# Head 7's searches ahead of its rows, eight rows ahead of its gates, no unit search or gelu inside the map stage, four tiles between heads 6 and 7

## What is computed

```
def peer_mixer(h, wq, subkeys, u, v):
    q = (h @ wq).reshape(B, S, PEER_HEADS, 2, PEER_HALF_DIM)          # 8 heads
    scores = jnp.einsum('bshcd,hcnd->bshcn', q, subkeys)               # 2 x 128 keys
    s_top, i_top = lax.top_k(scores, PEER_TOPK)                        # 16 of 128, twice
    cand = s_top[..., 0, :, None] + s_top[..., 1, None, :]             # 16 x 16 sums
    cand_idx = i_top[..., 0, :, None] * PEER_N_KEYS + i_top[..., 1, None, :]
    best, pos = lax.top_k(cand, PEER_TOPK)                             # 16 experts a head
    expert_idx = jnp.take_along_axis(cand_idx, pos, axis=-1)
    gates = jax.nn.softmax(best, axis=-1)
    a = jnp.einsum('cd,ced->ce', h, u[expert_idx])
    act = jax.nn.gelu(a, approximate=False) * gates
    return jnp.einsum('ce,ced->cd', act, v[expert_idx])
```

## Time and profile before

| | us |
|---|---|
| three runs, median | 3875.9 |
| three runs, lowest and highest | 3874.65, 3895.38 |
| the profiled execution | 3852.57 |
| its span | 3850.8 |
| TensorE busy | 3490.0 (91%) |
| VectorE busy | 2636.5 (68%) |
| GpSimd busy | 1382.5 (36%) |
| ScalarE busy | 982.7 (26%) |

### The profile page before, as it was taken

The page is one execution under the profiler, slowest core; times in us unless marked ns, Lnnn a source line. Parts: engine busy times, 40 slices in busy tenths (PEclk is TensorE's granted clock), DMA queues, the critical chain, the costliest instruction groups (busy, mean ns, idle before and its releaser), DMA issues.

```text
span 3850.8 us, 50373 instructions
## 1 busy us (share of the span) xinstructions
PE 3490.0 (91%) x13726; PEld 2235.0 (58%) x13726; DVE 2636.5 (68%) x5617; ACT 982.7 (26%) x2147; POOL 1382.5 (36%) x1220
## 2 busy tenths in 40 slices
PE   4998998999956999999978989989997689999997
PEld 2554445776754448874445544467767544688643
DVE  6656016898898777677566640289899987777774
ACT  1433102322263003330023330123323610133200
POOL 0000002444424565566400000044454256566662
PEclk9999999999978999999989989999998889999999
DMA  6322215888756999899942322178877589999997
GB/s 239 140 103 77 98 61 188 322 311 313 275 180 241 404 401 390 330 388 388 374 183 104 109 85 90 61 260 331 313 286 260 180 306 401 402 377 337 390 392 296
DMA packets 274015, 999.71 MB, mean 260 GB/s; under 512 B 31353, under 2 KB 48249, under 8 KB 262785
## 3 DMA queue, kind: packets, MB, share of 16 engines
q0 software_dynamic: 153600, 553.72, 38.2%
q1 hardware_dynamic: 120194, 443.42, 30.5%
HBM read 971.85 MB, written 25.17 MB: 259 GB/s over the span
## 4 chain that ended last, share of the span: by engine, by line
PE 65%; DVE 22%; issue 4%; DVEq 4%; DMA 3%; ACT 2%; ACTq 0%; POOL 0%; SPq 0%; POOLq 0%
PE ps L605 23%; PE ps L558 12%; PE ps L785 9%; DVE mod L1431 4%; DVE arena L1425 4%; PE ps L516 3%; PE ps L548 3%; PE ps L613 3%; PE ps L493 2%; DMA arena<-in_u_dram,idx 2%; PE ps L636 1%; DVE mod L1445 1%; PE ps L525 1%; PE ps L589 1%; DVE arena L1321 1%
## 5 line engine op out<-in xcount | busy, mean ns | idle before, releaser
L1167 POOL DMA_INDIRECT arena<-in_u_dram,idx x512 | 656.1, 1281 | 984.7 <-issue 652.3
L558 PE MATMUL ps<-hT,mod 128*128 128x256 f32 x4096 | 929.0, 381 | 0.0
L605 PE MATMUL ps<-arena 128*128 128x512 f32 x2048 | 881.5, 594 | 3.7 <-ACT hT L963 3.7
L1167 POOL DMA_INDIRECT arena<-in_v_dram,idx x512 | 630.2, 1231 | 632.2 <-DVE mod L1431 369.6
L558 PEld LDWEIGHTS ps<-hT,mod 128*128 128x128 f32 x4096 | 762.4, 191 | 92.1
L1425 DVE CUSTOM_DVE_ANT_0 arena<-arena 128x1024 f32<-128x1024 f32 x512 | 617.1, 1226 | 232.7 <-DMA arena<-in_u_dram,idx 229.5
L1431 DVE SCALAR_TENSOR_TENSOR mod<-arena,mod 128x1024 f32<-128x1024 f32 x512 | 657.3, 1284 | 121.4 <-DMA arena<-in_v_dram,idx 91.6
L605 PEld LDWEIGHTS ps<-arena 128*128 128x128 f32 x2048 | 390.4, 191 | 492.3 <-issue 492.2
L979 ACT COPY mod<-ps 128x512 f32<-128x512 f32 x512 | 274.6, 590 | 553.2 <-PE ps L548 553.2
L548 PE MATMUL ps<-const,arena 128*128 128x128 f32 x2048 | 269.1, 275 | 17.8 <-ACT mod L979 16.6
L548 PEld LDWEIGHTS ps<-const,arena 128*128 128x128 f32 x2048 | 239.0, 141 | 49.1 <-ACT mod L979 23.9
(11 more groups left out here) (202 smaller groups left out, 3477.2 us busy)
## 6 DMA issues: line engine op xcount, KB each, us to landing
arena<-in_u_dram SPq DMA_DIRECT2D x256, 512.0 KB, 6.9
arena<-in_v_dram SPq DMA_DIRECT2D x256, 512.0 KB, 6.8
arena<-in_ada_w_dram SPq DMA_DIRECT2D x56, 1024.0 KB, 4.9
arena<-in_w_qkv_dram SPq DMA_DIRECT2D x48, 512.0 KB, 5.6
arena<-in_w_m_dram SPq DMA_DIRECT2D x16, 1536.0 KB, 6.6
arena<-in_w_q_dram SPq DMA_DIRECT2D x32, 576.0 KB, 6.3
gate_scratch<-hT SPq DMA_DIRECT2D x64, 256.0 KB, 2.2
hT<-gate_scratch POOLq DMA_DIRECT2D x128, 128.0 KB, 8.1
```

The costliest lines, as they stand in the source:

```text
L558: last = pe.matmul(ps[:, 6 + tile // 2 % 2, tile % 2 * NT:(tile % 2 + 1) * NT], u_turned[:, tile % 2, k * P:(k + 1) * P], hT[:, k, DT0:SEQ ...
L605: last = pe.matmul(ps[:, 2 * c + n, :], act_t[:, e, c * P:(c + 1) * P], stream[:, slot, n * 512:(n + 1) * 512], start=(half == 0 and e == ...
L1167: pool.indirect_dma_start(out=ring[:, r % RING, :], out_offset=None, in_=table, in_offset=bass.IndirectOffsetOnAxis(ap=idx[:, j % 4, k:k + ...
```

## The change

A table `ENDS` says after which tile each head stands: eight tiles behind each of heads 0 to 4, four behind head 5, four behind head 6, 16 behind head 7. SyncE's loads, TensorE's and ScalarE's lists follow it. VectorE does both searches of head 7 before any of its rows, then eight rows (140 to 147), the gates, and the rows to 160 with unit 6's search; the maps begin at row 161 instead of 164 and take 31 rows with 32 batches, so row 192, with unit 7's search, falls behind the last batch. ScalarE's exponential and gelu of unit 5 move from batch 16 to behind the last batch.

```diff
+ENDS = [0, 8, 16, 24, 32, 40, 44, 48]
+G_ROW = 161
+G_END = 192
...
-                for hd in range(HEADS - 2):
+                for hd in range(HEADS - 1):
                     load_q(hd + 1)
-                    more_u(8 * hd + 4, 8)
-                load_q(HEADS - 1)
-                more_u(HALF - 12, 12)
+                    first = STREAM + ENDS[hd]
+                    more_u(first, (STREAM + ENDS[hd + 1] if hd < HEADS - 2 else HALF) - first)
...
-                    if hd < HEADS - 2:
-                        act_tiles(l, 0, 8 * hd, 8 * hd + 8)
-                act_tiles(l, 0, 8 * (HEADS - 2), HALF)
+                    if hd < HEADS - 1:
+                        act_tiles(l, 0, ENDS[hd], ENDS[hd + 1])
+                act_tiles(l, 0, ENDS[-1], HALF)
...
-                    if b == 16:
-                        unit_gates(l, 5)
                 keep_batch(l, NB - 1)
-                for j in range(6, 9):
+                for j in range(5, 9):
                     unit_gates(l, j)
...
-            def gate_maps(l, row0):
+            def gate_maps(l):
...
-                    rows(l, row0 + b, row0 + b + 1)
+                    rows(l, G_ROW + b, min(G_ROW + b + 1, G_END))
...
-                for hd in range(HEADS):
+                for hd in range(HEADS - 1):
...
+                topk_dense(l, HEADS - 1, 0)
+                topk_dense(l, HEADS - 1, 1)
+                rows(l, 20 * (HEADS - 1), 20 * (HEADS - 1) + 8)
                 gates_dense(l, BLOCKS - 1).then_inc(S["pre_done"], 1)
-                rows(l, 160, 164)
+                rows(l, 20 * (HEADS - 1) + 8, G_ROW)
                 dve.wait_ge(S["pq_ev"], ND * l + ND)
                 park()
-                gate_maps(l, 164)
-                rows(l, 196, KEEP0)
+                gate_maps(l)
+                rows(l, G_END, KEEP0)
```

6 lines of the change are left out of this document (3 added, 3 removed).

## The result

The changed kernel takes 3842.6 us (median of 20 runs, 3829.8 to 3884.0), the one before 3877.3 us in the same session (20 runs, 3855.0 to 3908.8). The ratio is 0.9921, with a 95% interval of 0.9898 to 0.9944: some 31 us faster (22 to 40), where 30.8 were forecast. The profiled executions are 3850.8 and 3834.4 us long, 16 apart and not 31, since one execution of this kernel scatters by 20 us and more. So the time is compared by the ratio of many executions, and the profiles are compared by stages.

What follows compares the result with a forecast made beforehand. VectorE was taken to bound the map stage and its start, TensorE the value tiles behind; 3.4+12.0 = 15.4 us a layer, 30.8 for both, gave 3875.9-30.8 = 3845 us, range 3826 to 3866.

Steps and rivals of the forecast that it cites:

- Inside the map stage: Map stage: unit 7's search (9.7 us) and unit 5's gelu wait (2.25 us) move behind it, 12.0 us a layer gained.
- Start of the maps: First `columns` at 1056.5 instead of 1059.88, 2 us of late rows included: 3.4 us a layer, bounds -1.1 to 5.4.
- the wait of 8.75 us: ScalarE's wait for head 7's second search before the last gates' exponential; removed by doing the searches ahead of the rows.
- the weight wait of 6.8: TensorE's 6.79 us wait for head 7's query weights right behind head 6; four tiles between the heads cover that load.
- the low clock: TensorE's slowed tile 61, 6.9 us where 4.33 is usual; the 2.6 us loss was to go with the wait before it.
- The new wait at head 6: ScalarE's exponential for heads 4 and 5 waits for head 5's second search; TensorE stands 4.5 us, perhaps 2.6 more at low clock.
- One row less in the map stage gives nothing: Map stage with 31 rows instead of 32: no gain, as the last batch waits for its matmuls, not a row.
- Behind the map stage: Moved work makes row 200 5 us later by the clock, 21 against TensorE; counted as nothing, 0 to 5 us a layer lost.
- (b): VectorE's lag returns at the kept maps' second part or the reload of x: 5 to 6 us a layer, 3856; chance 0.15.
- (a): The gather can't follow before the maps; start 1.1 us later than before, 10.9 us a layer gained, 3854; chance 0.14.
- (c): Slower: kept-map rows cost the DMA pace, TensorE stands 19 us, 7 us a layer more than gained, 3890; chance 0.04.
- (d): Tile 60's exponential still ends at 1041.81; maps start 8.2 us late, 3.8 us a layer left, 3868; chance 0.04.

Runs made afterwards that it cites:

- p2: Kernel before with only the map stage's part changed: rows 164 to 191, unit 5's gelu and unit 7's search behind it; ratio to the kernel before 0.9932.
- s1: Changed kernel with eight more rows put behind the map stage (row end 184 instead of 192), kept parts unmoved; ratio to the kernel before 0.9862.
- p4: The changed kernel once more, unaltered, on the same chip as its separately tested parts; ratio to the kernel before 0.9928.
- q4: Changed kernel with unit 5's gelu and its two table loads back inside the map stage after batch 16; ratio to the kernel before 0.9915.
- q1: Changed kernel with unit 6's gates and search right behind the last gates, ahead of the twelve rows; ratio to the kernel before 0.9939.
- p1: Kernel before with only head 7's two searches ahead of its rows and eight rows ahead of the gates; ratio to the kernel before 1.0034.
- r1: Changed kernel with three useless top-key searches (some 8.5 us of VectorE) right behind the maps; ratio to the kernel before 0.9982.
- s3: Changed kernel with the map stage's row end at 184 and both kept parts eight rows sooner; ratio to the kernel before 0.9904.

## Why the prediction was right, and which step was off

- **What bounds the kernel.** Right: VectorE sets the map stage and its start, TensorE the stages behind. p2 and s1 show it by taking VectorE's work out: 28.7 and 42.9 us won by the timelines, 26.5 and 53.5 timed.
- **The total.** 30.8 us forecast, 30.6 timed. That it agrees so closely is luck: the timelines show 26.6 up to the first value matmuls, the interval is 22 to 40 us, and the start's term was too large.
- **Inside the map stage, 12.0 us.** Right: 12.6 and 11.0 in after, 12.6 and 12.1 in p4. For the gelu's 2.25 q4 has 1.82 and 2.49, and the stage as a whole 2.7.
- **Start of the maps, 3.4 us.** This term was mis-sized: 1.0 and 2.0 in after, 1.5 and -0.2 in p4, and 0.3 when the mean of all twelve starts with this code is set against those of before and p2. In layer 0 of after the step was "Between 3.2 and none I take 2" for late rows; it was 4.3. The issues were no slower than reckoned; the rows came 9.3 to 11.6 us behind them. That the two searches in a row had let the transfers run dry, and all then came at once, fits the DMA view and was not tested by itself. In p4 and q1 the rows were less late and VectorE waited for the exponential instead (2.2 to 3.8 us), where the prediction's own times leave 0.9. The bounds given (-1.1 to 5.4) held.
- **What the start was credited to.** Here the reasoning went wrong though the sum did not. I wrote the wait of 8.75 us, the weight wait of 6.8 and the low clock off as costs to be removed. They were TensorE's and ScalarE's waits; VectorE's own work in that stretch is the same in either order but for three rows. The start could win those 3.9 us less the idle time that VectorE gets in return (2.5 in layer 0 of after), and the three rows come back in the map stage. p2 has none of these edits and is as fast.
- **The new wait at head 6.** Forecast 4.5 us with or without the low clock; 0.67 on ScalarE and 1.66 on TensorE in layer 0 of after, at full clock. What I had left out is that ScalarE's copies for head 6 come late (2.83 us), which hides most of it there. Where they do not, as in the four layers named under q4, the wait comes out larger than forecast, 5.5 to 7.9 us on TensorE.
- **One row less in the map stage gives nothing.** Right: the last batch of after waits 1.68 us for TensorE's matmuls, where that of before, with a row ahead of it, waited 0.48. It doesn't hold for more rows: eight less gave 7.2 us in layer 0 and 9.0 to 10.8 in layer 1.
- **Behind the map stage, nothing.** Right but for one layer: none in layer 1 of after, p4 and q1; in layer 0 of after the wait of 4.02 us and the low clock behind it cost 7.3, more than the 5 allowed for and about rival (b)'s 5 to 6. The lag of VectorE at row 200 was forecast 5 us by the clock; it was 592.6 against 587.0 us after the first row, 5.6. The row that was priced at some 2.1 us took 2.0 to 2.1 behind the kept maps (98.9 us for the last 48 in s1). That s1 moved eight rows more there and lost nothing at the kept maps, and that VectorE stood 20 and 25 us there in p4, says that in most executions there is room for this lag.
- **The rivals.** (a): the gather fell behind by 4.3 us, not by the 6.6 that would have made the start late. (b): once, with 7.3 us. (c): no. (d): not in after; p1 shows its mechanism, a late exponential with twelve rows and a search behind it, with 10.8 us a layer where (d) had 8.2.

What stays open: whether r1's 0.4 to 0.6% are more than scatter and, if so, where they go, as its 8.5 us of VectorE time lie at a place with 100 us to spare; and how much of the difference between s3 and s1 is more than scatter.

## What to carry to other kernels

Where one engine sets a stretch, add up that engine's busy and idle time from the stretch's start to its end before pricing any edit: an edit counts if it takes work out of the sum or idle time out of it, and waits of other engines inside it are costs only where they make that engine wait. Then look for the stretch where that engine waits for transfers anyway and move work there until another engine sets the first one; here each row moved was worth about 1 us, and eight more than the change moved were still worth it (`G_END = 184`, 0.9862). Before moving a step ahead of its queue, look at what it waits for: 16 rows too early turned a wait of 4 us on TensorE, seen in one layer of one execution, into 32 us of waiting on VectorE. And look at a wait in a second execution before you tune for it.
